# The first up chunk of the last layer: token tiles stationary and 512 weight columns moving, with a turn afterwards

## The reference

```python
def conv_ffn(h, w_up, conv_w, conv_b, w_down):
    u = h @ w_up                                   # 256 x 1024 by 1024 x 5632
    up = jnp.pad(u, ((0, 0), (1, 1), (0, 0)))
    u = up[:, :-2] * conv_w[0] + up[:, 1:-1] * conv_w[1] + up[:, 2:] * conv_w[2] + conv_b
    a, g = jnp.split(u, 2, axis=-1)
    return (a * jax.nn.silu(g)) @ w_down

o = merge_branches(y_ml, y_ga, y_na, zg, w_branch[l], w_out[l])
x = x + ga1 * rms_norm_2(o, g_post_mix[l])
f = conv_ffn(modulate(rms_norm_2(x, g_pre_ffn[l]), sh2, sc2), w_up[l], conv_w[l], conv_b[l], w_down[l])
x = x + ga2 * rms_norm_2(f, g_post_ffn[l])
```

## Time and profile before

| | |
|---|---|
| median of 3 runs | 1776.18 us (1775.14 to 1778.1) |
| the profiled execution | 1772.2 us, its span 1770.3 us |
| granted TensorE clock, mean of that execution | 0.993 |
| PE busy | 1703.3 us, 96% |
| DVE busy | 1255.9 us, 71% |
| ACT busy | 841.9 us, 48% |
| second layer's up chunk 0, first matmul | 1560.63 us |
| its up chunk 1, first matmul | 1586.51 us |

### The profile page before, as it was taken

The page is one execution under the profiler, slowest core; times in us unless marked ns, Lnnn a source line. Parts: engine busy times, 40 slices in busy tenths (PEclk is TensorE's granted clock), DMA queues, the critical chain, the costliest instruction groups (busy, mean ns, idle before and its releaser), DMA issues.

```text
span 1770.3 us, 25663 instructions
## 1 busy us (share of the span) xinstructions
PE 1703.3 (96%) x10056; PEld 1459.1 (82%) x10056; DVE 1255.9 (71%) x2200; ACT 841.9 (48%) x1360; POOL 0.2 (0%) x4
## 2 busy tenths in 40 slices
PE   7989989999999999999999999999999999999998
PEld 7878878777788778889888888888778889989987
DVE  7889766774779698856877775257746776667874
ACT  6665444554334444344444442346463455546653
POOL 0000000000000000000000000000000000000000
PEclk9999999999999999999999999999999999999999
DMA  8546433232125344532435555224222343535553
GB/s 330 217 155 226 168 127 111 70 133 66 54 84 173 113 146 175 204 107 87 152 126 193 199 197 178 95 73 143 79 77 72 126 149 122 189 103 183 190 183 116
DMA packets 71976, 251.77 MB, mean 142 GB/s; under 512 B 7984, under 2 KB 12336, under 8 KB 71216
## 3 DMA queue, kind: packets, MB, share of 16 engines
q1 hardware_dynamic: 66384, 241.74, 39.6%
q10 hardware_dynamic: 5472, 8.39, 1.4%
HBM read 249.05 MB, written 1.05 MB: 141 GB/s over the span
## 4 chain that ended last, share of the span: by engine, by line
PE 77%; DVE 14%; ACT 5%; issue 3%; DMA 0%; ACTq 0%; DVEq 0%
PE bank L650 63%; DVE w_lo L1655 4%; PE bank L780 3%; PE bank L959 2%; PE bank L945 2%; PE bank L1036 2%; PE bank L936 1%; ACT w_hi L1124 1%; PE bank L743 1%; PE bank L1025 1%; DVE mod_w L1710 1%; DVE att L2193 1%; DVE probT L1710 0%; DVE resid_x L2072 0%; PE bank L889 0%
## 5 line engine op out<-in xcount | busy, mean ns | idle before, releaser
L1655 DVE TENSOR_TENSOR w_lo<-w_raw,w_hi 128x1024 fp32r<-128x1024 f32 (+1 forms) x356 | 424.6, 1210 | 257.5 <-ACT w_hi L1124 256.0
L1124 ACT ACTIVATE w_hi<-w_raw 128x1024 fp32r<-128x1024 f32 (+1 forms) x356 | 365.6, 1045 | 327.1 <-PE bank L650 288.3
L650 PE MATMUL bank<-hT_hi,w_hi 128*128 128x512 f32 (+1 forms) x1280 | 446.6, 349 | 5.3 <-DVE w_lo L1655 4.1
L650 PE MATMUL bank<-hT_hi,w_lo 128*128 128x512 f32 (+1 forms) x1280 | 438.0, 342 | 0.0
L650 PE MATMUL bank<-hT_lo,w_hi 128*128 128x512 f32 (+1 forms) x1280 | 437.8, 342 | 0.0
L650 PEld LDWEIGHTS bank<-hT_hi,w_hi 128*128 128x128 f32 x1280 | 242.9, 190 | 34.2 <-ACT w_hi L1124 4.5
L650 PEld LDWEIGHTS bank<-hT_hi,w_lo 128*128 128x128 f32 x1280 | 242.9, 190 | 28.3
L650 PEld LDWEIGHTS bank<-hT_lo,w_hi 128*128 128x128 f32 x1280 | 243.1, 190 | 26.9 <-issue 1.0
L1710 DVE SCALAR_TENSOR_TENSOR mod_w<-mod_w,c_rows 128x1024 f32<-128x1024 f32 x96 | 116.9, 1218 | 1.5 <-DMA mod_w<-in_mod_weights 1.5
L650 PE MATMUL bank<-w_hi,hT_hi 128*128 128x512 f32 x272 | 114.3, 420 | 1.4 <-DVE gkT_lo L2233 1.4
L650 PE MATMUL bank<-w_lo,hT_hi 128*128 128x512 f32 x272 | 106.8, 393 | 0.0
(11 more groups left out here) (373 smaller groups left out, 2892.7 us busy)
## 6 DMA issues: line engine op xcount, KB each, us to landing
w_raw<-in_weights SPq DMA_DIRECT2D x356, 512.0 KB, 4.1
mod_w<-in_mod_weights SPq DMA_DIRECT2D x96, 512.0 KB, 3.9
nbias<-in_window_bias ACTq DMA_DIRECT2D x32, 128.0 KB, 2.8
resid_c<-in_ctx ACTq DMA_DIRECT2D x2, 1024.0 KB, 5.7
c_rows<-in_conditions SPq DMA_DIRECT2D x1, 1024.0 KB, 5.7
gatew<-in_gate_weights SPq DMA_DIRECT2D x1, 1024.0 KB, 11.6
decay<-in_decay SPq DMA_DIRECT2D x1, 1024.0 KB, 5.6
out<-resid_x ACTq DMA_DIRECT2D x2, 512.0 KB, 2.6
```

The costliest lines, as they stand in the source:

```text
L650: mm = pe.matmul(held[key][:, oc], st, mv_, start=(opens and k == 0 and t == 0 and i == 0), stop=(closes and k == tiles - 1 and t == 2), s ...
L1124: a.activation(w_hi[:, p % RING, :, used], w_raw[:, p % RING, :].rearrange("p (k n) -> p k n", k=KP)[:, :, used], ACT.Copy).then_inc(hi_re ...
L1655: v.tensor_tensor(w_lo[:, p % RING, :, used], w_raw[:, p % RING, :].rearrange("p (k n) -> p k n", k=KP)[:, :, used], w_hi[:, p % RING, :, ...
```

## The change

Chunk 0 of the last layer's up product is computed the other way round: `gemm_by_groups` gets one bank for each token tile (key `upt`, pool "acc"), the tile's tokens stationary and 512 weight columns moving. ACT copies the two banks to the new tile `up_tok` in SBUF. `turn_up`, a step laid beside chunk 1 after that chunk's first 12 matmuls, waits for both copies and turns the 8 blocks of 128x128 on PE into the two banks ("up", l, 0) in the arrangement that they had before; from there on ACT and DVE go on as before. The two banks are taken from "rot". The turn of "rot" isn't set back any more in the last layer. The first layer's order is unchanged. `gemm` gets an argument for the pool, so that chunk 1, which now has work beside it, still takes its banks from "rot".

```diff
+    up_tok = sb("up_tok", [P, NT, COLS], R + 84 * KB)
...
             def gemm(banks, tiles, x_hi, x_lo, weights_stationary, beside=None, inputs=None,
-                     by_bank=False, first_k=0, opens=True, closes=True):
+                     by_bank=False, first_k=0, opens=True, closes=True, pool=None):
...
-                pool = "gemm" if beside else "rot"
+                pool = pool or ("gemm" if beside else "rot")
...
-                if gi and which == "ffn":
+                if gi and which == "ffn" and l != LAYERS - 1:
                     turn["rot"] -= KD // 2
...
                 norm_T(l, "ffn", 0)
-                up = blocks_T(("up", l, 0), 4, None, qs)
-                gemm_by_groups([(key, "acc" if g < 2 and not last else "rot", subs, True) for g, (key, subs) in enumerate(up)], l, "ffn")
+                def turn_up():
+                    for t in q_tts:
+                        pe.wait_ge(*drained_at((("upt", l), t)))
+                    for g in range(2):
+                        ps = take(pe, (("up", l, 0), g))
+                        for j in range(2):
+                            for n, t in enumerate(q_tts):
+                                mm = pe.transpose(ps[:, (2 * j + n) * P:(2 * j + n + 1) * P],
+                                                  up_tok[:, n, (2 * g + j) * P:(2 * g + j + 1) * P], ident)
+                        mm.then_inc(*filled((("up", l, 0), g)))
+                    yield
+
+                if last:
+                    gemm_by_groups([((("upt", l), t), "acc", [(slice(0, COLS), slice(0, COLS), slice(t * P, (t + 1) * P))], False)
+                                    for t in q_tts], l, "ffn")
+                    turned = Beside(turn_up())
+                else:
+                    up = blocks_T(("up", l, 0), 4, None, qs)
+                    gemm_by_groups([(key, "acc" if g < 2 else "rot", subs, True) for g, (key, subs) in enumerate(up)], l, "ffn")
+                    turned = None
                 for c in range(1, FB // 2):
-                    gemm_T(("up", l, c), qs, hT_hi, hT_lo)
+                    gemm_T(("up", l, c), qs, hT_hi, hT_lo, beside=turned if c == 1 else None, pool="rot")
...
                 output(l, "mix", "wo", q_tts, gain_mix, (l, "ffn"))
                 per = 512 // nq
+                if last:
+                    for t in q_tts:
+                        key = (("upt", l), t)
+                        ahead(key)
+                        act.wait_ge(*filled_at(key))
+                        a.activation(up_tok[:, t - NT, :], psum(key)[:], ACT.Copy).then_inc(*A.drain(key))
                 for c in range(FB // 2 + lag):
```

## The result

The changed kernel is faster: the median of 4 executions is 1763.78 us (1761.6 to 1769.95), of the kernel before on the same chip 1775.66 us (1773.87 to 1778.1); the ratio is 0.9941, 95% interval 0.9916 to 0.9967. A second timing on another chip gave 1765.09 us (6 executions) against 1775.28 us (29), ratio 0.9936, 0.9918 to 0.9955.

The account below looks back on a forecast made before the run. PE was taken to bound the kernel, busy for 96% of the span. Chunk 0's saving of 8.6 us less 0.9 for transposes gave 7.7, so 1776.2 became 1768.5 us, range 1766.0 to 1772.5.

Parts of the forecast that it names:

- the prices: PE matmuls of chunk 0: 192 at 0.111 us become 48 at 0.227, 10.5 us less on paper.
- the walk: PE followed matmul by matmul through chunk 0 with its waits: chunk 1 starts at 1577.9, not 1586.51, 8.6 us earlier.
- transposes and copies: Eight transposes on PE's path add 0.9 us; ACT's two copies fit its idle time and cost nothing.
- The margin for tile 3's copy: ACT's copy finishes 0.7 us before PE asks; without cover the wait would be 0.7 or 1.7 us.
- No piece of weights came late: Chunk 1's first split weights ready at about 1576.3, before its start at 1577.9; no cost.
- the rivals: Weight feed binds (0.10); clock or matmul price eats most gain (0.08); slower (0.03); operand order makes no difference in PE time.
- the turn: Not setting back the bank pool's turn after the second `norm_T` causes no bank wait and costs nothing.
- I take one such stretch, and at the same place: One half-clock stretch assumed in changed chunk 0, covering 10 `norm_T` matmuls and 1.2 us of piece 2.
- Bounds: Best and worse cases for the changed kernel: 1767.3 us up to 1770.1, or 1770.8 with a late copy.
- Best: the clock never falls: No half clock in the changed chunk 0: group 1 ends at 1576.7, gain 8.9 us, 1767.3.
- my 7.7: Predicted total saving in us: 8.6 from chunk 0 less 0.9 for the transposes.
- the range: Predicted time between 1766.0 and 1772.5 us, said to leave out less than 2 in 10.

Follow-up runs that it names:

- after_again: The changed kernel timed again without edit on another chip: 1765.09 us against 1775.28 for the kernel before, ratio 0.9936.
- the filled version: The kernel before with PE's two gaps in group 0 of chunk 0 filled by unread 512-column matmuls: 1773.98 us against 1773.94, ratio 0.9996.
- turn_back3: The changed kernel with the turn of the bank pool set back as in the kernel before: 1764.52 us against 1773.94, ratio 0.9946.
- turn_only: The kernel before with only the set-back of the bank pool's turn left out in the last layer: 1778.84 us against 1775.28, ratio 1.0015.
- null_before: The kernel before, unchanged, timed against itself: 1773.99 us against 1775.28, ratio 0.9994.

## Why the prediction was right and where it failed

**Right: the prices.** 48 matmuls of 512 columns at 0.23 us for 192 of 128 at 0.111; the 128-column version gives the whole gain back. In the changed kernel the wide matmuls start 0.23 us apart (after_again: 22 distances from 1571.55 to 1576.56 us, 0.228 each).

**Right: the walk.** Laid on the common start of before and after_again: the second `norm_T` at 1566.20 (said 1566.25); the gap before piece 1 1.89 us (said about 2.1); chunk 1 at 1576.95. I had said 1577.9 with one stretch of half clock and 1576.7 with none, and there was none: 0.25 us off. Group 1 begins at 1571.21, as said (1571.2). Behind it its first two matmuls start 0.34 us apart and not 0.227, and the chain counts chunk 1 from 1576.95, where PE's timeline has its first matmul at 1576.78; together that is the quarter. I had expected chunk 1 8.6 us earlier; against the profile with one stretch it came 9.6 us earlier. From chunk 1's start to the end it is 0.9 us longer, as said: 1761.6 - 1576.95 = 184.65 against 1770.3 - 1586.51 = 183.79.

**Right: transposes and copies.** 0.87 us by the chain, and as much again when doubled. The margin for tile 3's copy was 0.6 us (1584.15 to 1584.78; said 0.7), and taking the cover away cost 0.73 us of waiting (said 0.7 to 1.7). No piece of weights came late: in after_again PE has no wait from the second `norm_T` (1566.20) up to 1600 us. None of the rivals came true.

**Right, but for less than it seemed: the turn.** Costed at nothing, and nothing it is in the changed kernel. My reading of the banks would have been wrong for the kernel before, where the same line costs a wait of 1.68 us.

**Wrong: the clock, in two places.** The step "I take one such stretch, and at the same place" put 1.2 us on the changed kernel that six profiles of its wide forms don't show. So no run shows that term of the sum, 10 matmuls of `norm_T` and 1.2 us of piece 2 at half clock in the changed kernel. What the runs show is such a stretch in the kernel before (3.4 us at 0.50, the 16 `norm_T` matmuls in 3.45 us, 0.216 each; elsewhere in it, 512 columns at 0.43 us), and in after_again a clock of 1.00 from 1557 to 1577 us, with `norm_T` in 2.05 us. The larger mistake is in "Bounds": "Best: the clock never falls", gain 8.9. It varied the clock on the side of the changed kernel only and held the kernel before at the one stretch of its one profile. Five profiles of before have 0, 1, 1, 3 and 3 of them, so the saving is 7.7, 8.6 or 11.5 us, by execution, on the mean of the five 217.5 - 207.9 = 9.6 us. That is also the distance between the means of the timed executions, 1774.8 us (60 of before, all but the first four) and 1765.2 us (10 of the changed kernel); with ten executions that spread over 8 us, and five profiles over 3.9, neither is sure to better than about 2 us. That my 7.7 equals the saving with no half clock on either side (215.59 - 207.9) is luck: it was summed with one stretch on both. The least sure link is the filled version, whose times didn't follow its profile. With 9.6 taken from the 1776.2 us that I started from, the forecast would have been 1766.6.

**Too narrow: the range.** Half of the rest, 1766.6 to the measured 1763.78, lies in the start value: 1776.2 was the median of three executions, and the mean of the 60 later ones is 1774.8, 1.4 us less. The other half, 1.4 us, is between the changed kernel's mean of 1765.2 us and the median of its first four. Single executions spread wider: stretches of half clock in earlier stages go with a later tile 2's residual, 1551.2 to 1553.7 us in the five profiles with six of them (of 3.4 us each) ahead of it, 1560.2 us in the one with twelve. The changed kernel's ten executions lie between 1761.6 and 1769.95. I allowed for the median's spread 1.3 us below my best case; the second timing's own median, 1765.09, lies below my range as well, so the range was at fault and not only the draw.

## What to carry to other kernels

In this kernel, where each matmul loads its own weights, its price hardly depended on the columns up to 256 (0.111 us at 128, 0.120 at 256, 0.227 at 512), so where that is measured, make the moving side wide, and pay transposes for it if they are few (eight cost 0.87 us here). Price the clock on both sides of a comparison: take several profiles of the kernel before, and measure a stage from a common instruction in front of it. And a line that gives back a turn of banks can be free in one form of the code (turn_back3) and cost a wait in another (1.68 us in turn_only); look at who holds the bank that comes next.

## What the runs showed of the hardware

The same program with the same gaps (1.48 and 0.65 us) had, in one stage, 0, 3.4 or 10.2 us of half clock, from one execution to the next; in the profiles before and null_before, with 3.4 and 10.2 us, the first `norm_T` (1557.10) and piece 0 (1560.63) start at the same hundredth. The 10.2 us came only with 128 columns moving; six profiles with 256 or 512 columns had none in that stage, in spite of gaps of 1.48 and 1.85 to 1.91 us. But three of the eight profiles with 128 columns had none there either, so that the width keeps the clock up is a likely reading and not a shown one.

At half clock (granted 0.50 in both stretches) 128 and 256 columns cost the same. Starts of null_before, 19 distances (0.213 us each), then of turn_only, 13 distances (0.213 us each):

```profile
1565.03 0.41 PE L780 MATMUL bank<-hT_lo,w_hi 128*128 128x128 f32 x1
1569.08 0.41 PE L780 MATMUL bank<-hT_hi,w_lo 128*128 128x128 f32 x1
```

```profile
1587.85 0.42 PE L650 MATMUL bank<-hT_lo,w_hi 128*128 128x256 f32 x1
1590.62 0.38 PE L650 MATMUL bank<-hT_hi,w_lo 128*128 128x256 f32 x1
```

With 512 columns it is 0.43 us. So each width takes a little under twice its price at full clock (0.111, 0.120, 0.227; 1.92, 1.78 and 1.89 times), also where the columns can't be what fills the time, since 256 cost nearly what 128 do.

In the kernel before one stretch is worth 1.0 us (216.57 less 215.59) where it falls mostly on a `norm_T` that would have waited, and 10.2 us of half clock cost 2.9 us more than 3.4 (219.4 less 216.6).
